# A chain of two transformer blocks on one Trainium2 core: gated linear attention normalises each head as it ends, the delta rule masks its first two groups earlier, and the last feed-forward starts its second product one chunk sooner

## The chip, the cores and the metric

The kernel runs on one core of one Trainium2 chip. The metric is the device time of one execution in microseconds (us), as the median of the runs shown. "About no change" below means within 0.2% of the time before.

## The reference

One sequence of 256 tokens, width 1024, float32, goes through two blocks. The first block is two layers: dilated window attention with a gated feed-forward ("layer a"), then gated linear attention with a gated feed-forward ("layer b"). The second block ("layer c") is attention beside a bidirectional gated delta rule, and a feed-forward with a convolution of three taps over the tokens. Three of these parts matter here.

```python
# layer b, for each of 4 heads (keys 128 wide, values 256), chunks of 64 tokens, forwards and backwards
o = chunked_linear_attention(q * exp(b), k * exp(-b), v)        # + states carried from chunk to chunk
y = rms_norm(o, out_norm) * silu(r)                             # norm over the 256 values of a head
h = h + y @ w_out
# layer c, delta rule: (I + A)^-1 of each 128 x 128 block, by levels of 2, 4, ... 64
# layer c, feed-forward
u = dwconv_centred(h @ w_up, conv_w, conv_b);  g, val = split(u);  h = (silu(g) * val) @ w_down
```

## The kernel before, in words

The program is written out by hand for each engine: TensorE (PE), VectorE (DVE), ScalarE (ACT), GpSimd (POOL) and SyncE (SP), whose queue loads the weights. Every engine runs its own list in order, and semaphores with fixed counts connect the lists. What order of work an engine has is therefore what is written in the code.

**Weights.** Every weight matrix is cut into halves of 128 x 2048 float32 (two 512 KB transfers each). A half is loaded into one of four slots `raw`, ACT copies it rounded to a short format into one of three slots `whi` (`Weights.hi`, L191), DVE subtracts the two into `wlo` (`Weights.lo`, L197), and PE multiplies with both (L326 to L328: three products for one). A slot is filled again when PE has signalled `used` for the half that stood in it. SP issues the loads.

**Layer b.** `project_pe/act/dve` make q, k, v and r (ACT applies silu to r while it takes it from PSUM, L1372) and the decays e1, e2, e3. Then `heads_pe/act/dve` run over the 4 heads. For head h, DVE makes `qd, kd, ke` (six products of 128 x 256, L1510 to L1512). PE transposes `ke` (L1445) and makes the scores (L1451), then works on a chunk of the modulation weights that has nothing to do with the head (`M.acc`, L827 and L828, 16 matmuls of 512 columns), then the products of keys and values of the chunks (L1464) and a few small ones (`M.cols`, L842). DVE masks the scores (L1519), carries the states over the chunks (L1527, L1530), makes `wlo` for the two halves that come next (L197), and once PE has made the head's output (L1472, L1478) copies it from PSUM to `o` (L1540). ACT copies the transposes (L1492), the row of the modulation product (L835), and the two halves (L191).

After the fourth head comes the gate (`gate_act`, `gate_dve`): a square over all of `o` (L1552), a sum over each head (L1559), a root (L1554), a reciprocal, and three products over 128 x 2048 (L1565 by the scale, L1567 by the gain, L1569 by silu(r)). Then PE transposes the result (L408) and multiplies by the output weights.

**Delta rule** (`gdn_heads`). It has two phases of four groups. For each group DVE makes the matrix N (its last step is L2398), POOL multiplies it by the mask of the first level (L2502), and DVE makes the first X with `first` (L2405). Then `levels` goes over 24 steps: `level_masks` on DVE makes two masked copies of a group's X (L2411, L2412), PE transposes one (L2220) and makes two products, with a third masked matrix that POOL makes (L2524), and DVE subtracts. Step s works on group s mod 4.

**Feed-forward** (`ffn`, used in all three layers). The first product runs over 11 chunks; chunk ci uses PSUM banks 0 to 3 if ci is even, 4 to 7 if it is odd. DVE ends each with `val` (L753), counted in `ff_val`, and splits it into `hid` (ACT L721, DVE L756). Then the second product ("down") runs over 6 double halves into banks 4, 5 and then 6, 7. In layer c, and there alone, the argument `beside` is None: nothing is done by PE between the two products.

## Time and profile before

| | |
|---|---|
| median of 3 runs | 1881.06 us (1879.68 to 1881.2) |
| profiled execution: its own time | 1878.88 us |
| its span in the trace | 1877.3 us |
| PE matmul busy | 1693.8 us (90%) |
| DVE busy | 1139.8 us (61%) |
| ACT busy | 863.8 us (46%) |
| POOL busy | 243.8 us (13%) |

How to read it: the span is from the first instruction to the last. The 1.58 us between it and the execution's own time lie around it. The busy time of PE is a model of pipelined matmuls, so a busy PE need not be PE at its fastest: the column PEclk (granted clock) says at which share of 2.4 GHz it ran.

### The profile page before, as it was taken

The page shows a single profiled execution, that of the slowest core. Times are in us where ns is not written, and L with a number is a line of the kernel's source. Part 1 is how long each engine was busy: PE and PEld are TensorE (multiplying, and loading weights), DVE is VectorE, ACT ScalarE, POOL GpSimd, SP SyncE. Part 2 cuts the span into 40 slices and gives each one's busy share as a digit, 9 for nine tenths or more (in the row PEclk, how much of TensorE's full clock was granted, in tenths as well). Part 3 has the DMA queues.
Part 4 walks back from the last instruction along what each step waited for, and adds up shares of the span by engine and source line. Part 5 has one row for each costly group of instructions (what it writes and reads, how often), then busy time and mean ns, then how long its engine had stood idle before and what let it go on. Part 6 is the DMA issues. An engine that isn't in the chain of part 4 may idle for free. (4 is left out here: it accounts for less than half of the span.)

```text
span 1877.3 us, 25093 instructions
## 1 busy us (share of the span) xinstructions
PE 1693.8 (90%) x10106; PEld 1472.9 (78%) x10106; DVE 1139.8 (61%) x1464; ACT 863.8 (46%) x1059; POOL 243.8 (13%) x205
## 2 busy tenths in 40 slices
PE   4999999989999987589999999988979899989988
PEld 3777888879987865479988678767879878779976
DVE  3887666755554454645546775347887565567754
ACT  5344556644433553244444423364544554345542
POOL 1653240000000000000000610004444100000000
PEclk9999999989999998799999999988989899989999
DMA  5552445645555343146645404100000155445533
GB/s 201 173 177 98 135 133 181 202 128 180 185 167 195 127 157 122 58 157 183 191 155 168 137 1 138 45 17 1 1 1 1 46 181 179 157 146 179 178 126 123
DMA packets 161906, 240.97 MB, mean 128 GB/s; under 512 B 12640, under 2 KB 80992, under 8 KB 161664
## 3 DMA queue, kind: packets, MB, share of 16 engines
q1 hardware_dynamic: 154400, 232.81, 38.1%
q10 hardware_dynamic: 7104, 4.64, 0.9%
q8 instruction: 81, 1.33, 0.3%
q0 software_dynamic: 288, 1.92, 0.3%
q14 instruction: 33, 0.27, 0.0%
HBM read 238.29 MB, written 1.05 MB: 127 GB/s over the span
## 5 line engine op out<-in xcount | busy, mean ns | idle before, releaser
L197 DVE TENSOR_TENSOR wlo<-raw,whi 128x2048 fp32r<-128x2048 f32 x224 | 524.3, 2352 | 309.3 <-ACT whi L191 298.8
L191 ACT ACTIVATE whi<-raw 128x2048 fp32r<-128x2048 f32 x224 | 420.4, 1887 | 302.3 <-PE ps L328 258.1
L326 PE MATMUL ps<-xs,whi 128*128 128x256 f32 (+1 forms) x1312 | 387.4, 295 | 18.3 <-DVE xs L460 7.7
L327 PE MATMUL ps<-xs,whi 128*128 128x256 f32 (+1 forms) x1312 | 386.0, 294 | 0.0
L328 PE MATMUL ps<-xs,wlo 128*128 128x256 f32 (+1 forms) x1312 | 385.8, 294 | 0.0
L326 PE MATMUL ps<-whi,xs 128*128 128x512 f32 x672 | 275.8, 410 | 19.0 <-DVE wlo L197 11.2
L326 PEld LDWEIGHTS ps<-xs,whi 128*128 128x128 f32 x1312 | 250.1, 191 | 27.2 <-issue 20.7
L327 PE MATMUL ps<-wlo,xs 128*128 128x512 f32 x672 | 270.7, 403 | 0.0
L328 PE MATMUL ps<-whi,xs 128*128 128x512 f32 x672 | 270.1, 402 | 0.0
L327 PEld LDWEIGHTS ps<-xs,whi 128*128 128x128 f32 x1312 | 250.2, 191 | 5.7
L328 PEld LDWEIGHTS ps<-xs,wlo 128*128 128x128 f32 x1312 | 250.0, 191 | 5.8
L326 PEld LDWEIGHTS ps<-whi,xs 128*128 128x128 f32 x672 | 129.8, 193 | 53.0 <-issue 21.1
L328 PEld LDWEIGHTS ps<-whi,xs 128*128 128x128 f32 x672 | 129.2, 192 | 32.1
L327 PEld LDWEIGHTS ps<-wlo,xs 128*128 128x128 f32 x672 | 129.7, 193 | 29.2
L326 PE MATMUL ps<-whi,hid 128*128 128x512 f32 x264 | 106.0, 402 | 8.7 <-DVE wide L753 8.7
L327 PE MATMUL ps<-wlo,hid 128*128 128x512 f32 x264 | 105.4, 399 | 0.0
L328 PE MATMUL ps<-whi,hid 128*128 128x512 f32 x264 | 105.4, 399 | 0.0
L1673 POOL TENSOR_TENSOR wide<-cst,wide 128x128 f32<-128x128 f32 x4 | 3.5, 870 | 765.5 <-DMA wide<-in_rows 765.5
L928 POOL TENSOR_TENSOR wide<-wide 128x512 f32<-128x512 f32 (+1 forms) x30 | 54.0, 1822 | 132.0 <-DVE wide L915 83.3
L933 POOL TENSOR_TENSOR wide<-wide 128x512 f32<-128x512 f32 (+1 forms) x30 | 67.8, 2281 | 2.6 <-DVE wide L915 1.7
L326 PEld LDWEIGHTS ps<-whi,hid 128*128 128x128 f32 x264 | 50.2, 190 | 21.2 <-DVE wide L753 9.1
L328 PEld LDWEIGHTS ps<-whi,hid 128*128 128x128 f32 x264 | 50.2, 190 | 12.3
(366 smaller groups left out, 2394.3 us busy)
## 6 DMA issues: line engine op xcount, KB each, us to landing
raw<-in_ffn_w_gate_up SPq DMA_DIRECT2D x88, 512.0 KB, 4.7
raw<-in_a_w_in SPq DMA_DIRECT2D x72, 512.0 KB, 4.6
raw<-in_w_in SPq DMA_DIRECT2D x60, 512.0 KB, 4.6
raw<-in_w_mod SPq DMA_DIRECT2D x48, 512.0 KB, 4.6
raw<-in_w_up SPq DMA_DIRECT2D x44, 512.0 KB, 4.7
raw<-in_ffn_w_down SPq DMA_DIRECT2D x40, 512.0 KB, 4.5
raw<-in_b_w_in SPq DMA_DIRECT2D x24, 512.0 KB, 4.6
raw<-in_w_down SPq DMA_DIRECT2D x20, 512.0 KB, 4.1
```

What stands on the lines that cost most here:

```text
L191: self.hi_ok.inc(act.activation(self.whi[:, h % NHI, 0:nk, :], self.raw[:, h % NRAW, 0:nk, :], ACT.Copy))
L197: self.lo_ok.inc(dve.tensor_tensor(self.wlo[:, h % NRAW, 0:nk, :], self.raw[:, h % NRAW, 0:nk, :], self.whi[:, h % NHI, 0:nk, :].bitcast(F ...
L326: pe.matmul(o, ahi, bhi, start=start, stop=False)
L327: pe.matmul(o, ahi, blo, start=False, stop=False)
L328: return pe.matmul(o, alo, bhi, start=False, stop=stop)
L928: i_ = pool.tensor_tensor(self.av[:, t], self.xv[:, t], bc(cos[:, t, :], 1, self.nh), ALU.mult)
L933: i_ = pool.tensor_tensor(dst(t), self.av[:, t], dst(t) if self.bv is None else self.bv[:, t], ALU.add)
L1673: pool.tensor_tensor(tab[:, 0, t, :], cosv[:, t, :], gain, ALU.mult)
```

## The change

There are three edits.

1. Layer b. The three arrays `qd, kd, ke` get two buffers each. `scale_qk(0)` is made during the projections, and `scale_qk(h + 1)` directly after the states of head h, in front of the `wlo` splits. The head's output is no longer copied to `o`: ACT squares it straight from PSUM with a running sum (2 instructions of 128 x 256 a head) and takes the root, DVE takes the reciprocal and makes one product from PSUM with the scale and with r (2 of 128 x 256 a head), into r itself. The gain is multiplied into r before, by POOL, in two instructions. The whole gate after the heads is gone.
2. Delta rule. In each phase `level_masks` for steps 0 and 1 stand in front of the last `first` and no longer behind it.
3. Feed-forward of layer c. In front of the second product PE waits for `val` of the tenth chunk, not of the eleventh.

```diff
-            pe.wait_ge(ff_val.sem, v0 + N_FFC)
+            pe.wait_ge(ff_val.sem, v0 + N_FFC - (beside is None))
...
+        def scale_qk(h):
+            hs = slice(h * SEQ, (h + 1) * SEQ)
+            qd, kd, ke = qd_[h % 2], kd_[h % 2], ke_[h % 2]
+            for d in range(2):
+                dve.tensor_tensor(qd[:, d, :], qT[:, h, :], e1[:, d, hs], ALU.mult)
+                dve.tensor_tensor(kd[:, d, :], kT_[:, h, :], e2[:, d, hs], ALU.mult)
+                i_ = dve.tensor_tensor(ke[:, d, :], kT_[:, h, :], e3[:, d, hs], ALU.mult)
+            lb_qk.inc(i_)
...
-            for h in (*later[4], *later[5]):
+            for h in later[4]:
+                W.lo(h)
+            dve.wait_ge(lb_ex.sem, 1)
+            dve.wait_ge(lb_evac.sem, 2)
+            scale_qk(0)
+            for h in later[5]:
                 W.lo(h)
...
+                for t in range(TT):
+                    act.wait_ge(lb_o.sem, 2 * h + t + 1)
+                    as_.inc(act.activation(sq[:, t], ps[:, 6 + t, 0:GLA_DV], ACT.Square, scale=GLA_DV ** -0.5, accum_out=st[:, h, t:t + 1]))
+                act.wait_ge(as_.sem, as_.n)
+                lb_rt.inc(act.activation(st[:, h], st[:, h], ACT.Sqrt, bias=eps_col))
+
+        def heads_pool():
+
+            pool.wait_ge(rows_in.sem, rows_at)
+            for j in range(2):
+                pool.wait_ge(lb_evac.sem, 5 + j)
+                half = slice(j * CW, (j + 1) * CW)
+                lb_gr.inc(pool.tensor_tensor(r[:, :, half], r[:, :, half], bc(gain[:, half], 1, TT), ALU.mult))
...
+                if h + 1 < GLA_HEADS:
+                    scale_qk(h + 1)
+                M.out(8 + h, 5)
                 for half in nxt[h]:
                     W.lo(half)
-                M.out(8 + h, 5)
+                dve.wait_ge(lb_rt.sem, h + 1)
+                vs.inc(dve.reciprocal(st[:, h], st[:, h]))
+                dve.wait_ge(vs.sem, vs.n)
+                dve.wait_ge(lb_gr.sem, 1 + h // 2)
                 for t in range(TT):
-                    dve.wait_ge(lb_o.sem, 2 * h + t + 1)
-                    lb_out.inc(dve.tensor_copy(o[:, t, hv], ps[:, 6 + t, 0:GLA_DV]))
+                    lb_out.inc(dve.scalar_tensor_tensor(r[:, t, hv], ps[:, 6 + t, 0:GLA_DV], st[:, h, t:t + 1], r[:, t, hv],
+                                                        ALU.mult, ALU.mult))
...
-        gate_act()
-        gate_dve()
-        split_and_add(lambda t, k: o[:, t, k * P:(k + 1) * P], 0, out_chunks, nxt_chunk, norm)
+        heads_pool()
+        split_and_add(lambda t, k: r[:, t, k * P:(k + 1) * P], 0, out_chunks, nxt_chunk, norm)
...
                 if Gn % 4 == 3:
+                    if ph == 0:
+                        dve.wait_ge(gm_in.sem, 16)
+                    dve.wait_ge(gp_x.sem, 4 * ph + 2)
+                    level_masks(ph, 0)
+                    level_masks(ph, 1)
                     first(Gn)
```

VectorE before, between the outputs of head 1 and the masked scores of head 2 (L1530 ends the states, L197 are the splits of the next weights, L1540 the copies to `o`, L1510 to L1512 the six products that head 2 needs):

```order
L1530 SCALAR_TENSOR_TENSOR wide<-wide,ps 128x256 [waits s_dve_steps] x2
L197 TENSOR_TENSOR wlo<-raw,whi 128x2048 [waits s_hi_ok,s_raw_in0]
L197 TENSOR_TENSOR wlo<-raw,whi 128x2048 [waits s_hi_ok,s_raw_in1]
L851 TENSOR_TENSOR gcol<-ps,vec 128x4 [waits s_mod_cols]
L1540 COPY wide<-ps 128x256 [waits s_b_product] x2
L1510 TENSOR_TENSOR wide<-wide 128x256 [waits s_b_product]
L1511 TENSOR_TENSOR wide<-wide 128x256
L1512 TENSOR_TENSOR wide<-wide 128x256
```

VectorE in the changed kernel at the same kind of place, from the end of one head's states to the next head's masked scores (here L1387 to L1389 are the products, L1569 the product from PSUM into r):

```order
L1554 SCALAR_TENSOR_TENSOR wide<-wide,ps 128x256 [waits s_dve_steps] x2
L1387 TENSOR_TENSOR wide<-wide 128x256
L1388 TENSOR_TENSOR wide<-wide 128x256
L1389 TENSOR_TENSOR wide<-wide 128x256
L1387 TENSOR_TENSOR wide<-wide 128x256
L1388 TENSOR_TENSOR wide<-wide 128x256
L1389 TENSOR_TENSOR wide<-wide 128x256
L854 SCALAR_TENSOR_TENSOR modcol<-ps,vec 128x8 [waits s_mod_cols]
L197 TENSOR_TENSOR wlo<-raw,whi 128x2048 [waits s_hi_ok,s_raw_in2]
L197 TENSOR_TENSOR wlo<-raw,whi 128x2048 [waits s_hi_ok,s_raw_in3]
L1565 RECIPROCAL wide<-wide 128x2 [waits s_b_root]
L1569 SCALAR_TENSOR_TENSOR wide<-ps,wide 128x256 [waits s_b_gain,s_dve_steps]
```

The products for the next head have moved in front of the two splits and no longer wait for the head's output; the wait for ACT's root stands in front of the next head's masked scores.

VectorE before, at the end of the fourth head and in the gate (L1559 to L1569), up to the split of the result into `xs` (L453):

```order
L851 TENSOR_TENSOR gcol<-ps,vec 128x4 [waits s_mod_cols]
L1540 COPY wide<-ps 128x256 [waits s_b_product] x2
L1559 TENSOR_REDUCE wide<-wide 128x8 [waits s_rope_out,s_b_out,s_b_squares,s_mod_rows,s_b_product]
L1562 RECIPROCAL wide<-wide 128x8 [waits s_rows_in,s_b_root]
L1565 TENSOR_TENSOR wide<-wide 128x2048 [waits s_dve_steps]
L1567 TENSOR_TENSOR wide<-wide 128x2048 [waits s_dve_steps]
L1569 TENSOR_TENSOR wide<-wide 128x2048 [waits s_dve_steps]
L453 TENSOR_TENSOR xs<-ps,xs 128x512 [waits s_rope_out,s_dve_steps,s_xs_hi,s_b_root,s_b_product]
```

The same place in the changed kernel:

```order
L851 TENSOR_TENSOR gcol<-ps,vec 128x4 [waits s_mod_cols]
L197 TENSOR_TENSOR wlo<-raw,whi 128x2048 [waits s_hi_ok,s_raw_in2]
L197 TENSOR_TENSOR wlo<-raw,whi 128x2048 [waits s_hi_ok,s_raw_in3]
L1565 RECIPROCAL wide<-wide 128x2 [waits s_b_root]
L1569 SCALAR_TENSOR_TENSOR wide<-ps,wide 128x256 [waits s_b_gain,s_dve_steps]
L1569 SCALAR_TENSOR_TENSOR wide<-ps,wide 128x256
L453 TENSOR_TENSOR xs<-ps,xs 128x512 [waits s_b_gain,s_b_out,s_xs_hi,s_b_root,s_b_product]
```

Four instructions over 2048 elements are gone from between the last output and the split; a reciprocal and two of 256 elements stand there.

VectorE in the changed kernel at the end of the second phase's (and likewise the first phase's) preparation in the delta rule (L2402 ends N, L2414 is `first`, L2420 and L2421 are the level masks):

```order
L2402 TENSOR_TENSOR wide<-wide,spare 128x512 [waits s_dve_steps,s_gdn_scales]
L2420 TENSOR_TENSOR spare<-wide 128x512 [waits s_gdn_x_first,s_gdn_masks_in]
L2421 TENSOR_TENSOR spare<-wide 128x512
L2420 TENSOR_TENSOR spare<-wide 128x512
L2421 TENSOR_TENSOR spare<-wide 128x512
L2414 TENSOR_TENSOR wide<-cst,wide 128x512 [waits s_gdn_n_first]
L2420 TENSOR_TENSOR spare<-wide 128x512 [waits s_gdn_u,s_gdn_x_first]
```

Before, the last `first` (L2405 there), with its wait for POOL, stood directly behind N, and all the masks behind it.

## Rows read from the trace of the kernel before

**Rows 1.** The page, busy time of each engine and its instructions.
```profile
PE 1693.8 (90%) x10106; PEld 1472.9 (78%) x10106; DVE 1139.8 (61%) x1464; ACT 863.8 (46%) x1059; POOL 243.8 (13%) x205
```

**Rows 2.** Waits of PE: us in total, times, longest.
```profile
PE ps L2220 <- DVE spare L2412: 17.7, 2, 9.9
...
PE ps L1445 <- DVE wide L1512: 15.2, 4, 5.0
PE ps L408 <- DVE wide L1569: 14.0, 1, 14.0
```

**Rows 3.** Timeline of PE, heads: start, us, instruction, [idle before].
```profile
699.56 0.95 PE L1445 MATMUL ps<-cst,wide 128*128 128x128 f32 x4 [5.05 <-DVE wide L1512]
...
739.00 1.12 PE L1445 MATMUL ps<-cst,wide 128*128 128x128 f32 x4 [3.78 <-DVE wide L1512]
...
741.47 0.77 PE L827 MATMUL ps<-whi,by_hi 128*128 128x512 f32 x1
...
746.49 2.75 PE L1464 MATMUL ps<-wide 128*128 128x256 f32 x12
...
752.20 0.67 PE L1472 MATMUL ps<-wide 128*128 128x256 f32 x2 [2.18 <-issue]
...
754.45 1.08 PE L1478 MATMUL ps<-wide 128*64 128x256 f32 x6
```

**Rows 4.** Timeline of DVE, end of head 2.
```profile
751.10 1.00 DVE L1530 SCALAR_TENSOR_TENSOR wide<-wide,ps 128x256 f32<-128x256 f32 x2
752.02 4.49 DVE L197 TENSOR_TENSOR wlo<-raw,whi 128x2048 fp32r<-128x2048 f32 x2
...
757.16 0.41 DVE L1510 TENSOR_TENSOR wide<-wide 128x256 f32<-128x256 f32 x1
...
758.83 0.42 DVE L1512 TENSOR_TENSOR wide<-wide 128x256 f32<-128x256 f32 x1
```

**Rows 5.** ACT: two timeline rows of layer b, one group by form.
```profile
694.55 1.02 ACT L1372 ACTIVATE wide<-ps 128x1024 f32<-128x1024 f32 x1 [3.62 <-PE ps L328]
...
782.14 0.30 ACT L1554 ACTIVATE wide<-wide,small 128x8 f32<-128x8 f32 x1 [1.15 <-DVE wide L1559]
...
L431 ACT ACTIVATE xs<-ps,vec 128x256 fp32r<-128x256 f32 x24 | 9.0, 482 | 0.0
```

**Rows 6.** Timeline of DVE and PE, end of head 3 and gate.
```profile
772.39 4.49 DVE L197 TENSOR_TENSOR wlo<-raw,whi 128x2048 fp32r<-128x2048 f32 x2
...
789.91 3.65 PE L408 MATMUL ps<-cst,wide 128*128 128x128 f32 x16 [14.02 <-DVE wide L1569]
```

**Rows 7.** Timeline of DVE, PE and ACT, between the feed-forward's products, layer c.
```profile
1795.08 4.49 DVE L197 TENSOR_TENSOR wlo<-raw,whi 128x2048 fp32r<-128x2048 f32 x2 [1.12 <-ACT whi L191]
...
1804.48 0.79 PE L326 MATMUL ps<-whi,hid 128*128 128x512 f32 x1 [7.32 <-DVE wide L753]
...
1806.99 2.29 DVE L197 TENSOR_TENSOR wlo<-raw,whi 128x2048 fp32r<-128x2048 f32 x1 [1.11 <-ACT whi L191]
...
1812.53 1.92 ACT L191 ACTIVATE whi<-raw 128x2048 fp32r<-128x2048 f32 x1 [5.64 <-PE ps L328]
1818.15 1.91 ACT L191 ACTIVATE whi<-raw 128x2048 fp32r<-128x2048 f32 x1 [3.70 <-PE ps L328]
```

**Rows 8.** Timeline of DVE and POOL, ends of the delta rule's preparations.
```profile
1284.81 1.56 DVE L2405 TENSOR_TENSOR wide<-cst,wide 128x512 f32<-128x512 f32 x1 [1.21 <-POOL wide L2502]
...
1287.79 0.68 DVE L2412 TENSOR_TENSOR spare<-wide 128x512 f32<-128x512 f32 x1
...
1377.38 1.57 DVE L2412 TENSOR_TENSOR spare<-wide 128x512 f32<-128x512 f32 x1
...
1284.73 2.59 POOL L2524 TENSOR_TENSOR spare<-wide,cst 128x512 f32<-128x512 f32 x2
```

**Rows 9.** Windows: start:end, length, busy and count per engine, PEclk, DMA share, GB/s.
```profile
714.00:717.00 3.00, 2.94 (x8) 1.10 (x8) 2.69 (x5) 0.00 (x0) 0.00 (x0) 0.53 0.00 1
...
732.00:735.00 3.00, 3.00 (x16) 1.41 (x16) 3.00 (x2) 0.00 (x0) 0.00 (x0) 1.00 0.14 53
```

More of the change, by code:

```diff
@@ L1274, in build @@
     lb_g, lb_ke, lb_att, lb_kv, lb_o = (Signal(nc, "pe", "b_" + n) for n in ("gates", "ke_transposed", "scores", "kv", "product"))
-    lb_ln, lb_ex, lb_evac, lb_kt, lb_sq = (Signal(nc, "act", "b_" + n) for n in ("gate_ln", "decays", "evacuated", "kt", "squares"))
-    lb_qk, lb_at, lb_s, lb_out, lb_sum = (Signal(nc, "dve", "b_" + n) for n in ("qk_scaled", "masked", "states", "out", "sum"))
+    lb_ln, lb_ex, lb_evac, lb_kt = (Signal(nc, "act", "b_" + n) for n in ("gate_ln", "decays", "evacuated", "kt"))
+    lb_qk, lb_at, lb_s, lb_out = (Signal(nc, "dve", "b_" + n) for n in ("qk_scaled", "masked", "states", "out"))
+    lb_gr = Signal(nc, "pool", "b_gain")
     lb_rt = Signal(nc, "act", "b_root")
@@ L1324, in layer_b @@
         dec = c(2, NB)
+        qd_, kd_, ke_ = ([c(2, SEQ) for _ in range(2)] for _ in range(3))
         at_ = Stage()
@@ L1505, in heads_dve @@
             for h in range(GLA_HEADS):
-                hs, hv = slice(h * SEQ, (h + 1) * SEQ), slice(h * GLA_DV, (h + 1) * GLA_DV)
+                hv = slice(h * GLA_DV, (h + 1) * GLA_DV)
                 if h:
                     dve.wait_ge(lb_o.sem, 2 * h)
-                for d in range(2):
-                    dve.tensor_tensor(qd[:, d, :], qT[:, h, :], e1[:, d, hs], ALU.mult)
-                    dve.tensor_tensor(kd[:, d, :], kT_[:, h, :], e2[:, d, hs], ALU.mult)
-                    i_ = dve.tensor_tensor(ke[:, d, :], kT_[:, h, :], e3[:, d, hs], ALU.mult)
-                lb_qk.inc(i_)
                 dve.wait_ge(lb_att.sem, h + 1)
```

30 lines of the change are left out of this document (2 added, 28 removed).

## The prediction

> **What bounds the kernel now.** I read the page first: PE is busy for 90% of the span [rows 1], so time can be won only where PE stands still or runs at half clock. Then the list of PE's waits, which names the places of this change: the masks of the delta rule (17.7 us in two waits, the longest 9.9), the six products in front of each head (15.2 us in four), the gate behind the heads (14.0 us) [rows 2]; the wait in front of the second product of the last feed-forward, 7.32 us, is read from the timeline [rows 7]. Last I read the timelines around each to see what DVE does while PE waits, and how late each following instruction would be.
>
> In layer b one head takes PE 20.3 us: transposes and scores 739.00 to 741.47, the modulation chunk to 746.49, keys times values and a wait of 2.18 us to 752.20, outputs to 755.53 (754.45 + 1.08), and 3.78 us of waiting for L1512 [rows 3]. In that last wait DVE finishes the splits it began at 752.02, copies the output and makes the six products, 757.16 to 759.25 [rows 4].
>
> **Head start.** The products of head 0 are now made before the last two splits of the projections. PE's list may go on when ACT has evacuated r, at 695.57 (694.55 + 1.02) [rows 5]; it started at 699.56 [rows 3]. I take 695.7, so 3.9 us earlier.
>
> **One head.** The six products (2.1 us, 757.16 to 759.25) stand directly behind the states, which end at 752.0 [rows 4]. They are ready at 754.1, before the outputs end at 755.53, so the 3.78 us are gone and PE goes from outputs to transposes in about 0.1. Without that gap I also expect more full clock: the 16 modulation matmuls took 5.0 us (741.47 to 746.49) with the gap ahead of them; 24 matmuls of the same size at full clock take 5.62 us (between the two ACT rows that wait for PE, 1812.53 and 1818.15 [rows 7]), 0.234 each, so 16 take 3.75. Transposes and scores took 2.47 at half clock; at full clock half of it, 1.24. I take the middle, 1.85, since some of it may still be slow. From keys times values to the outputs stays 5.71 (746.49 to 752.20), the outputs 3.33. Sum: 0.1 + 1.85 + 3.75 + 5.71 + 3.33 = 14.7 us in place of 20.3.
>
> What must keep up in these 14.7 us? Call A the end of a head's outputs; the states end at A - 3.5. DVE: products to A - 1.4, the small L854, two splits (4.5) to A + 3.2, reciprocal and two products from PSUM of about 0.5 each to A + 4.5, masked scores 1.0 to A + 5.5. Its next input, keys times values of the next head, ends at A + 0.1 + 1.85 + 3.75 + 2.75 = A + 8.4, so 2.9 us are left. The next modulation chunk wants the first new `wlo` at A + 2.0 and has it at A + 1.0, the second at A + 3.8 and has it at A + 3.2. ACT: a square of 128 x 256 from PSUM costs 0.48 [rows 5], the root 0.30, so with reading out the sum the root is there at about A + 1.2, and the copy of the transposes behind it is done some 3 us before keys times values need it; the table for roots is now loaded in head 0 and no longer in the gate. DMA moves next to nothing in stretches of the loop (share 0.00 and 0.14 [rows 9]), so weights are not what would be late.
>
> **POOL's two products with the gain.** They are new, and no row shows 128 x 1024 on POOL. Two of 128 x 512 take 2.59 us beside DVE [rows 8], so 2.6 each is my value; free would be the lower bound, and twice, 5.2, the upper. The first lies under the projections, the second starts at 695.6, when DVE clears its buffers. If DVE has to stand for it, the copy of the transposes is 2.6 us late, and it has 4 us of modulation matmuls as cover. Cost taken: 0; with 5.2 us it would be about 1.5.
>
> **Gate.** PE's gap after the last output is 14.02 us [rows 6]. What remains: the splits started 3.5 before A (772.39 against 775.89) and with the small operation ahead of them end at A + 1.1; root at A + 1.2; reciprocal 0.2, two products of 0.5, so PE starts at A + 2.7.
>
> Put together: last outputs at 695.7 + 4 x 14.7 = 754.5, transposes at 757.2 in place of 789.91: 32.7 us. From this I take one fall of the clock: in the four heads before, the 2.2 us gap that remains was followed by half clock once (714 to 717, clock 0.53) and not in head 1 (732 to 735, clock 1.00) [rows 9]; 3 us at 0.53 lose 1.4. The restart after a gap of 2.7 in place of 14 may keep some full clock, +0.4. Layer b: **31.7 us**, with bounds of 24 (a fall in every head, -5.6, and the POOL cost) and 35.
>
> **Delta rule.** DVE waited 1.21 us for POOL and then made `first` in 1.56, because POOL worked beside it; alone such an operation takes 0.68 [rows 8]. Now the masks use that wait. In phase 1 the first pair was complete at 1287.79 + 0.68 = 1288.5; it now starts at 1283.6 and with one of the two slowed is complete at 1285.9. But all eight masks of the first four steps and `first` are still DVE's work, POOL has the same three operations, and more of DVE's now fall beside them. So the first step starts 2.5 us earlier, the fourth hardly; PE's own steps decide what remains. I take 1.2 us. In phase 2 the first pair ended at 1379.0 (1377.38 + 1.57) and both of it were slowed; it loses the same wait and `first` ahead of it (1.21 + 1.56), so it would end near 1376.2, and PE's second step, which stood behind it, follows. I take 2.1. Together **3.3 us**, bounds 0 and 6.
>
> What speaks against this edit is the meeting of the two engines: the rows say 1.56 against 0.68 us for a DVE operation with two inputs beside POOL [rows 8]. The Trainium skill, page "SBUF — State Buffer", section on the two separate sides, says that such a DVE instruction and a GpSimd instruction that reads SBUF take a shared port pair as an exclusive lock for the whole instruction. By that rule every mask moved beside POOL waits out one POOL instruction and POOL in turn waits for it, and the edit gives nothing; the trace agrees so far as 1.56 is nearly one operation of each.
>
> **Feed-forward of layer c.** The second product's banks 4 and 5 are free after the tenth chunk. PE now starts at once, at about 1797.4: its last matmul ended at 1797.16 (1804.48 - 7.32), and the first split half was ready at 1797.3 (half of 1795.08 to 1799.57) [rows 7]. Two halves at 5.62 take it to 1808.7. The third half's `wlo` is ready at 1809.3 (1806.99 + 2.29), which does not depend on PE, so PE waits 0.6. Before, the third half began at 1818.1. That is **8.7 us**: 7.3 of waiting and 2.0 of half clock after it, less the new wait. Below: 7.0, if the clock falls again. The eleventh chunk's `hid` is wanted only by the fifth half, long after.
>
> **Sum.** 31.7 + 3.3 + 8.7 = 43.7 us. The profiled execution would go from a span of 1877.3 to 1833.6 and from 1878.88 to 1835.2; it lay 2.2 us under the median of the runs, so I forecast 1881.06 - 43.7 = **1837 us**.
>
> **Rivals.**
> - The clock, 0.15. PE falls to half clock after the remaining gap in every head and keeps it through the modulation chunk as now. For it: half clock at 714; against: full clock at 732 with the same gap [rows 9]. Each head then takes about 16.3 us: 1844 us.
> - The shared port, 0.10. DVE and POOL stop each other wherever they meet: the delta rule gains 0 and layer b pays 1.5. 1842 us.
> - DVE takes over as the bound of a head, 0.08. The reciprocal waits for ACT's root in front of the next masked scores. If DVE's list were 3 us longer than I count, its slack of 2.9 would be used up; if it were 6 us longer, three heads would lose about 3 us each: 1846 us.
> - Slower than before, 0.03. ACT's squares now stand behind the rounding of the next two halves, and DVE and the next head behind them. If a half lands late, both engines and PE stand, where before only the modulation chunk did. To turn 43.7 us of gain into a loss of over 3.8, each of four heads must be held 12 us, so halves would land more than 25 us after their slot came free. Against it: DMA shares of 0.00 and 0.14 [rows 9]. It would give 1890 us.
> - The edits do nothing that counts, since other work fills the same time, 0.02: 1881 us. Against it: PE has no other instruction before these waits.
> - My forecast, 0.62: 1832 to 1842.
>
> Within 0.2% (3.8 us) is what a measurement of this kernel can't tell from no change. The range 1830 to 1850 takes in the forecast, the first three rivals and a layer b that keeps clock fully. Faster 0.95, same 0.02, slower 0.03.
>
> **What would show it.** In the trace after: L1461 (the transposes of heads 1 to 3) starts within 0.2 us of the outputs' end, with a period near 14.7 us and DVE idle in front of L1551; PE's gap before L408 near 2.7; masks beside POOL at 1.5 us and PE's first level step 2 to 3 us after N; in the feed-forward no wait in front of the second product and one of about 0.6 in front of its third half. I am wrong if the period stays over 16.5, if the gap before L408 is over 5, or if the second product waits more than 3 us for its third half.

## The result and the profile after

The changed kernel takes 1834.8 us (median of 4 runs, 1830.42 to 1864.69) against 1880.37 us of the kernel before (4 runs, 1876.53 to 1881.2). The ratio is 0.9753, with a 95% interval of 0.9739 to 0.9767; the run of 1864.69 us had a disturbed clock and is not in the ratio. The profiled execution took 1835.56 us with a span of 1833.9 us, 43.4 us less than the span of before. The forecast was 1837 us, and the result lies in its range of 1830 to 1850.

The page's busy line, which answers to [rows 1]:

```profile
PE 1683.5 (92%) x10106; PEld 1462.5 (80%) x10106; DVE 1135.5 (62%) x1463; ACT 867.2 (47%) x1077; POOL 250.9 (14%) x207
```

PE executes the same 10106 matmuls, in 10.3 us less of busy time. So about a quarter of the 43.4 us is matmuls that ran at the faster clock; the rest is standing time. The list of PE's waits (us in total, times, longest) answers to [rows 2]:

```profile
PE ps L2224 <- DVE spare L2421: 14.5, 4, 6.2
...
PE ps L1488 <- issue: 6.5, 3, 2.2
...
PE ps L408 <- DVE wide L1569: 2.2, 1, 2.2
...
PE ps L326 <- DVE wide L753: 1.4, 1, 1.4
```

The 15.2 us for the six products are gone from it altogether, the 14.0 us of the gate are 2.2, the wait for L753 fell from 8.7 in two to 1.4 in one. The delta rule's wait is still there: 17.7 us in two waits have become 14.5 us in four.

**Heads.** Timeline of PE (start, us, instruction, idle before), which answers to [rows 3]: rows from heads 0 to 2 and the outputs of head 3.

```profile
697.59 0.63 PE L1461 MATMUL ps<-cst,wide 128*128 128x128 f32 x4 [1.16 <-issue]
...
713.24 0.66 PE L1461 MATMUL ps<-cst,wide 128*128 128x128 f32 x4
...
714.54 0.48 PE L827 MATMUL ps<-whi,by_hi 128*128 128x512 f32 x1
...
724.08 0.67 PE L1488 MATMUL ps<-wide 128*128 128x256 f32 x2 [2.18 <-issue]
724.68 1.08 PE L1494 MATMUL ps<-wide 128*64 128x256 f32 x6
...
727.33 0.66 PE L1461 MATMUL ps<-cst,wide 128*128 128x128 f32 x4
...
753.95 1.19 PE L1488 MATMUL ps<-wide 128*128 128x256 f32 x2 [2.18 <-issue]
...
758.13 1.97 PE L1494 MATMUL ps<-wide 128*64 128x256 f32 x6
```

L1461, the transposes, has no idle time before it in heads 1 to 3: PE goes from outputs to transposes at once. Head 1 ran at full clock throughout and took 727.33 - 713.24 = 14.09 us. What remains is the gap of 2.2 us before L1488, in which PE waits for the states. Behind it the same outputs take 3.25 us in head 1 (724.08 to 727.33) and 6.15 us in head 3 (753.95 to 758.13 + 1.97 = 760.10), since the groups are nearly twice as long there: 1.97 in place of 1.08 is half clock.

**DVE and POOL at the start.** Timeline of DVE and of POOL, around the products of head 0 and the clearing of the buffers, with the reciprocal at the end of head 0:

```profile
685.42 2.61 DVE L1387 TENSOR_TENSOR wide<-wide 128x256 f32<-128x256 f32 x1
687.96 0.41 DVE L1388 TENSOR_TENSOR wide<-wide 128x256 f32<-128x256 f32 x1
...
697.67 0.27 DVE L1529 MEMSET wide<- 128x256 f32 x1 [2.42 <-ACT wide L1374]
...
715.48 0.17 DVE L1565 RECIPROCAL wide<-wide 128x2 f32<-128x2 f32 x1 [0.70 <-ACT wide L1517]
...
685.19 2.56 POOL L1525 TENSOR_TENSOR wide<-wide 128x1024 f32<-128x1024 f32 x1 [411.09 <-ACT wide L1374]
697.57 2.38 POOL L1525 TENSOR_TENSOR wide<-wide 128x1024 f32<-128x1024 f32 x1 [9.82 <-ACT wide L1374]
```

The first product began 0.23 us after POOL's and took 2.61 us, its neighbour 0.41: it stood until POOL had ended. The clearing beside POOL's second product took its 0.27 us and was not held. The reciprocal of head 0 waited 0.70 us for ACT's root; in this head ACT loads the table for the root first, which takes it 1.28 us.

**Gate.** DVE and PE after the last output (at 760.10), which answers to [rows 6]:

```profile
760.99 0.17 DVE L1565 RECIPROCAL wide<-wide 128x2 f32<-128x2 f32 x1 [2.67 <-ACT wide L1517]
761.19 0.88 DVE L1569 SCALAR_TENSOR_TENSOR wide<-ps,wide 128x256 f32<-128x256 f32 x2
...
762.32 2.57 PE L408 MATMUL ps<-cst,wide 128*128 128x128 f32 x16 [2.22 <-DVE wide L1569]
```

**Delta rule.** DVE and PE after the last N of phase 1 (which ends at 1251.06) and of phase 2 (1341.30), which answers to [rows 8]:

```profile
1250.98 0.68 DVE L2420 TENSOR_TENSOR spare<-wide 128x512 f32<-128x512 f32 x1
1251.58 1.58 DVE L2421 TENSOR_TENSOR spare<-wide 128x512 f32<-128x512 f32 x1
...
1253.31 1.09 PE L2224 MATMUL ps<-cst,spare 128*128 128x128 f32 x4 [5.06 <-DVE spare L2421]
1256.22 1.12 PE L2224 MATMUL ps<-cst,spare 128*128 128x128 f32 x4 [1.82 <-DVE spare L2421]
1257.13 1.92 PE L2231 MATMUL ps<-spare 128*128 128x128 f32 x8
...
1262.69 0.69 DVE L2453 TENSOR_TENSOR wide<-wide,ps 128x512 f32<-128x512 f32 x1 [3.39 <-PE ps L2239]
...
1343.55 1.09 PE L2224 MATMUL ps<-cst,spare 128*128 128x128 f32 x4 [6.20 <-DVE spare L2421]
...
1353.43 0.69 DVE L2453 TENSOR_TENSOR wide<-wide,ps 128x512 f32<-128x512 f32 x1 [0.54 <-PE ps L2239]
```

The same places in the kernel before, where the last N ends at 1283.60 and 1373.20:

```profile
1288.62 2.23 PE L2220 MATMUL ps<-cst,spare 128*128 128x128 f32 x8 [7.82 <-DVE spare L2412]
1290.64 1.92 PE L2227 MATMUL ps<-spare 128*128 128x128 f32 x8
...
1295.40 0.69 DVE L2448 TENSOR_TENSOR wide<-wide,ps 128x512 f32<-128x512 f32 x1 [3.17 <-PE ps L2235]
...
1386.69 0.69 DVE L2448 TENSOR_TENSOR wide<-wide,ps 128x512 f32<-128x512 f32 x1 [1.34 <-PE ps L2235]
```

The first pair of masks is complete 2.1 us after N (1253.16 against 1251.06), where it took 4.9 us before (1288.47 against 1283.60). Three of the four masks that were moved take 1.58 us (two of them, at 1253.09 and 1254.59, are not shown), since each meets POOL. L2448, which is L2453 after, is the subtraction that ends a step.

**Feed-forward.** DVE and PE between the products, which answers to [rows 7]:

```profile
1760.04 4.49 DVE L197 TENSOR_TENSOR wlo<-raw,whi 128x2048 fp32r<-128x2048 f32 x2 [1.11 <-ACT whi L191]
...
1771.97 6.69 DVE L197 TENSOR_TENSOR wlo<-raw,whi 128x2048 fp32r<-128x2048 f32 x3 [1.11 <-ACT whi L191]
...
1762.48 0.47 PE L326 MATMUL ps<-whi,hid 128*128 128x512 f32 x1 [0.33 <-DVE wlo L197]
...
1774.41 0.47 PE L326 MATMUL ps<-whi,hid 128*128 128x512 f32 x1 [0.45 <-DVE wlo L197]
```

The wait of 7.32 us is one of 0.33 us, and the new wait before the third half is there, with 0.45 us.

**By stages.** The span is cut at five instructions that all kernels have: the end of r's copy from PSUM (before 695.57, after 697.49), the first L408 behind the heads (789.91, 762.32), the ends of the last N of phase 1 and of phase 2 (1283.60 and 1373.20, 1251.06 and 1341.30), and the end of the last `val` in the last feed-forward. Each number is a difference of two such times in that kernel's one profiled execution, the last one up to the end of the span.

| kernel | to r | heads and gate | to N, phase 1 | phase 1 | to last val | to the end | span |
|---|---|---|---|---|---|---|---|
| before | 695.57 | 94.34 | 493.69 | 89.60 | 431.23 | 72.87 | 1877.3 |
| after | 697.49 | 64.83 | 488.74 | 90.24 | 428.09 | 64.51 | 1833.9 |
| e1, layer b alone | 695.42 | 67.57 | 493.08 | 89.60 | 431.18 | 72.85 | 1849.7 |
| e2, delta rule alone | 695.71 | 94.35 | 493.68 | 90.95 | 426.40 | 72.91 | 1874.0 |
| e3, feed-forward alone | 695.55 | 96.22 | 493.82 | 89.60 | 431.20 | 64.51 | 1870.9 |
| e5, products early alone | 697.43 | 78.21 | 492.48 | 89.75 | 434.07 | 73.26 | 1865.2 |
| e6, after, products late | 697.27 | 88.29 | 487.55 | 88.34 | 427.71 | 64.54 | 1853.7 |
| e7, after, gap filled | 694.79 | 54.60 | 491.72 | 90.30 | 428.08 | 64.51 | 1824.0 |
| e8, after, one mask pair | 696.03 | 64.72 | 490.80 | 89.57 | 428.34 | 64.54 | 1834.0 |
| e9, after, POOL five times | 694.27 | 73.47 | 491.90 | 90.30 | 428.10 | 64.46 | 1842.5 |
| e10, e7 and e8 | 693.98 | 54.60 | 491.14 | 89.35 | 431.20 | 64.53 | 1824.8 |

Two columns differ where no edit can be the cause. The third holds no edit, and differs by up to 6.3 us. The first holds of the edits only the products of head 0 and POOL's first product, from 685 us on, and differs by up to 3.5 us. What the changed kernel lost there, 1.9 us, it had lost by 112 us, 1.6 of it between two of ACT's L191 (8.80 us, 102.77 to 111.57, where before it was 7.25, 102.30 to 109.55), as PE's matmuls of 0.40 us took 0.63 there. So the early products cost nothing in front of r.

Windows show what differs in the third stage, for 25 us that begin at about the same instruction in both kernels (start:end, length, busy and count for PE, PEld, DVE, ACT, POOL, then granted clock, DMA share, GB/s), first before:

```profile
1065.00:1090.00 25.00, 19.48 (x88) 12.72 (x87) 20.33 (x35) 7.28 (x15) 14.58 (x11) 0.84 0.20 70
```

and after:

```profile
1037.00:1062.00 25.00, 17.93 (x98) 12.15 (x97) 21.03 (x37) 7.29 (x15) 14.33 (x10) 1.00 0.19 65
```

The clock was 0.84 there and 1.00 here. What that was worth is read between two instructions that stand around it: from the start of ACT's L191 at 1062.49 to the next one at 1119.50 it was 57.0 us before, from 1034.15 to 1088.55 it was 54.4 after, so 2.6 us. Another 1.6 us was won in the 84 us in front of the last N of phase 1 (84.5 against 82.9, at a granted clock of 0.90 and 0.92). The remaining 0.7 us is the restart behind the gate: the first L408 group takes 2.57 us in place of 3.65 [rows 6], 1.1 less, but within the next 10 us 0.4 of it is lost again. That makes the 4.95 us that this stage gained. With layer b alone (e1) the stretch from L191 to L191 takes 57.0 us again, with the early products alone (e5) 56.1, with products late (e6) 54.4. It goes with none of the edits in an orderly way, and I count these 4.2 us as luck of the clock.

### The profile page after: what moved, and what is told of

It reads as the page before. It is cut to its first block and busy times, and to the rows that moved or that the text cites. A ratio compares the mean times of both kernels' runs of the same rounds, so it can differ in the third digit from the quotient of the medians.

```text
span 1833.9 us, 25119 instructions
## 1 busy us (share of the span) xinstructions
PE 1683.5 (92%) x10106; PEld 1462.5 (80%) x10106; DVE 1135.5 (62%) x1463; ACT 867.2 (47%) x1077; POOL 250.9 (14%) x207
## 5 line engine op out<-in xcount | busy, mean ns | idle before, releaser
L197 DVE TENSOR_TENSOR wlo<-raw,whi 128x2048 fp32r<-128x2048 f32 x224 | 524.1, 2352 | 298.9 <-ACT whi L191 288.4
L191 ACT ACTIVATE whi<-raw 128x2048 fp32r<-128x2048 f32 x224 | 420.6, 1888 | 294.9 <-PE ps L328 250.9
L1525 POOL TENSOR_TENSOR wide<-wide 128x1024 f32<-128x1024 f32 x2 | 4.9, 2466 | 420.9 <-ACT wide L1374 420.9
L328 PEld LDWEIGHTS ps<-whi,hid 128*128 128x128 f32 x264 | 49.7, 188 | 12.1
```

Source lines behind the costliest of these rows:

```text
L191: self.hi_ok.inc(act.activation(self.whi[:, h % NHI, 0:nk, :], self.raw[:, h % NRAW, 0:nk, :], ACT.Copy))
L197: self.lo_ok.inc(dve.tensor_tensor(self.wlo[:, h % NRAW, 0:nk, :], self.raw[:, h % NRAW, 0:nk, :], self.whi[:, h % NHI, 0:nk, :].bitcast(F ...
L328: return pe.matmul(o, alo, bhi, start=False, stop=stop)
L1525: lb_gr.inc(pool.tensor_tensor(r[:, :, half], r[:, :, half], bc(gain[:, half], 1, TT), ALU.mult))
```

## The experiments

**One edit each.** Three kernels take the change apart. e1 is the changed kernel with the other two edits undone:

```diff
-            pe.wait_ge(ff_val.sem, v0 + N_FFC - (beside is None))
+            pe.wait_ge(ff_val.sem, v0 + N_FFC)
...
-                    if ph == 0:
-                        dve.wait_ge(gm_in.sem, 16)
-                    dve.wait_ge(gp_x.sem, 4 * ph + 2)
-                    level_masks(ph, 0)
-                    level_masks(ph, 1)
                     first(Gn)
...
                 dve.wait_ge(gp_x.sem, 4 * ph + 4)
+                if ph == 0:
+                    dve.wait_ge(gm_in.sem, 16)
+                level_masks(ph, 0)
+                level_masks(ph, 1)
```

> The kernel before with the edit of layer b alone (nothing left out of the computation). Theory: nearly all of the gain is here. By the prediction's terms 31.7 us (1880.4 to about 1848.7); by the trace after, where the stretch from the end of r's evacuation to the transposes behind the gate is 64.8 us and was 94.3, 29.5 us there and 1 to 2 us of restart at full clock, 31. Rival (the DVE list or the shared port takes the gain back): 20 to 24 us. Three heads with half clock cost 1.6 to 2.9 us each in the trace after; I expect two to four of them again.

Measured: 1851.41 us, ratio 0.9856 (0.9837 to 0.9876), so 27.1 us (23.3 to 30.6). The heads and the gate took 67.57 us in place of 94.34, a gain of 26.8, and the restart kept 0.6 us of the third stage. That is 27.4, between the 31 of my theory and the 20 to 24 of the rival. The clock makes the difference to the changed kernel: here the outputs ran partly or wholly at half clock in all four heads (4.80, 4.85, 6.08 and 6.15 us, where the changed kernel has 4.80, 3.25, 4.85 and 6.15), which is 2.8 us.

e2 is the kernel before with the masks moved, and nothing else:

```diff
                 if Gn % 4 == 3:
+                    if ph == 0:
+                        dve.wait_ge(gm_in.sem, 16)
+                    dve.wait_ge(gp_x.sem, 4 * ph + 2)
+                    level_masks(ph, 0)
+                    level_masks(ph, 1)
                     first(Gn)
...
-                if ph == 0:
-                    dve.wait_ge(gm_in.sem, 16)
-                level_masks(ph, 0)
-                level_masks(ph, 1)
```

> The kernel before with the edit of the delta rule alone. The prediction's term was 3.3 us. The trace after speaks for less: the masks beside POOL took 1.57 us each, and the first phase, from the end of its last N to the end of the second phase's last N, took 90.2 us after and 89.6 before. So I now expect phase 1 to gain nothing (0 to -1) and phase 2 to gain 0 to 2: 0 to 1.5 us in all. The rival, my term of 3.3, would show as 1877.

Measured over 12 runs: 1875.92 us against 1878.94, ratio 0.9983 (0.9973 to 0.9993), so 3.2 us (1.3 to 5.1). So the time speaks for the 3.3 us of the prediction and not for the 0 to 1.5 that I expected here. By stages phase 1 took 1.35 us longer, and the stage with phase 2 4.8 us less. The first subtraction of a step came 0.5 us sooner behind N in phase 1 (11.27 against 11.80) and 2.0 us sooner in phase 2 (11.51 against 13.49); the rest of both differences lies later, where the granted clock differs.

e3 is the kernel before with the one wait changed:

```diff
-            pe.wait_ge(ff_val.sem, v0 + N_FFC)
+            pe.wait_ge(ff_val.sem, v0 + N_FFC - (beside is None))
```

> The kernel before with the earlier start of the last feed-forward's second product alone. The prediction's term: 8.7 us (7.3 of waiting, 2.0 of half clock, less a new wait of 0.6). Rival: the split of the third half ends later than PE reaches it by more than 3 us, and the gain is under 6.

Measured: 1872.21 us, ratio 0.9966 (0.9953 to 0.9979), so 6.4 us (3.9 to 8.8). Its own stage went from 72.87 to 64.51 us, 8.36 less, just as in the full change; 1.9 us were lost in heads and gate, where e3 has no edit.

The three add to 36.7 us and the full change is worth 46.4 us by its ratio ((1 - 0.9753) x 1880.37, 43.8 to 49.1). By their spans it is 37.3 against 43.4. The table shows where the other 6.1 us lie: the full change has 4.5 us more in the third stage than the three together and 4.6 more in heads and gate (29.5 against 26.8 in e1 and -1.9 in e3), 0.7 more in phase 1, and 1.9 and 1.8 less in the first stage and the one with phase 2. Where I read the rows, the clock accounts for them: one more head with slow outputs in e1 (2.8 us), half clock in the modulation chunk of head 0 in e3 (5.23 us in place of 4.39) and in the heads behind it, and the stretches of the third stage named above. So one profile's clock moves a stage by up to some 5 us.

**Layer b taken apart.** e5 is the kernel before with the products for the next head made early, in two buffers, and the old copy and gate kept:

```diff
+        def scale_qk(h):
+            ...
...
-        qd, kd, ke = c(2, SEQ), c(2, SEQ), c(2, SEQ)
+        c(6, SEQ)
...
                     lb_s.inc(i_)
+                if h + 1 < GLA_HEADS:
+                    scale_qk(h + 1)
+                M.out(8 + h, 5)
                 for half in nxt[h]:
                     W.lo(half)
-                M.out(8 + h, 5)
```

The old place of the six products stays reserved in e5. Without that (e4) `xs` shares a place with an array that PE still reads when DVE writes `xs`, so its result would hang on the timing, and it has no time.

> The kernel before with one part of the layer b edit: the six products are made ahead, in two buffers; the copies to o and the whole gate behind the heads stay. By rows 3 and 4: 3.9 us at the start, and 3.7 of waiting plus up to 1.9 of full clock for each of three heads, while the gate's 14.0 us stay: the stretch from r's evacuation to the transposes, 94.3 us before, would be 75 to 78, and the time 1880 less 16 to 20. Rival: the copies to o, behind the splits, hold PE's outputs, and the gain is under 12.

Measured: 1866.78 us, ratio 0.9928 (0.991 to 0.9947). That is 13.5 us by the ratio and 12.1 by the spans, where I expected 16 to 20. Heads and gate took 78.21 us, 16.1 less than before and at the edge of the expected 75 to 78; the other 4 us were lost where nothing is changed: 1.9 in front of r and 2.8 behind phase 1, less 1.2 won in the third stage. The timeline of PE in e5:

```profile
760.89 1.97 PE L1494 MATMUL ps<-wide 128*64 128x256 f32 x6
775.64 3.65 PE L408 MATMUL ps<-cst,wide 128*128 128x128 f32 x16 [12.78 <-DVE wide L1582]
```

The heads end at 762.86, so they took 65.4 us from r, where they took 80.3 before (775.89 - 695.57); the gate's gap is still 12.78 us.

e6 is the opposite: the changed kernel with its new normalisation, but the products at their old place behind the outputs.

```diff
                 if h:
                     dve.wait_ge(lb_o.sem, 2 * h)
+                    scale_qk(h)
...
-                if h + 1 < GLA_HEADS:
-                    scale_qk(h + 1)
```

> The changed kernel with the products for heads 1 to 3 made at their old place, behind the head's output and the new product into r; head 0's stay early. Theory: the gate's part of the gain stays (11 to 12 us) and the start (3.9), the per-head part goes and is more than gone, since the next products now also stand behind ACT's root: PE's gap in front of a head's transposes 4.5 to 5.5 us, where it was 3.8. Stretch 94.3 less 13 to 16, so 78 to 81; the time of the changed kernel plus 14 to 17. Rival: the gap is hidden and the time is within 5 us of the changed kernel.

Measured: 1858.28 us, ratio 0.9882 (0.9861 to 0.9902), with heads and gate at 88.29 us, 7 to 10 us more than I had expected (20 us more than the changed kernel by the spans, where I had 14 to 17). The timelines of PE and DVE in e6, head 1 to head 2, show why:

```profile
733.96 1.82 PE L1494 MATMUL ps<-wide 128*64 128x256 f32 x6
739.81 1.11 PE L1461 MATMUL ps<-cst,wide 128*128 128x128 f32 x4 [4.03 <-DVE wide L1389]
...
736.67 0.17 DVE L1564 RECIPROCAL wide<-wide 128x2 f32<-128x2 f32 x1 [1.43 <-ACT wide L1517]
...
737.66 0.42 DVE L1387 TENSOR_TENSOR wide<-wide 128x256 f32<-128x256 f32 x1
```

The products stand behind the wait for ACT's root, which did not exist before, so PE's gap is 4.03 us (5.31 behind head 0) in place of 3.78 [rows 3] (2.54 behind head 0). That adds 3.3 us, about as expected. What I had not counted is the outputs: they took 4.89, 4.91, 6.14 and 6.16 us, where before they took 4.91 and three times 3.32 or 3.33, so 7.2 us more at half clock.

So the per-head normalisation takes 11.8 us from the gate's gap, and the heads take 86.1 us (697.27 to 783.35) in place of 80.3, although e6 keeps the early start of head 0, which is worth 3.9. The two parts of the edit need each other. Early products alone bring 16.1. Normalisation with only the early start of head 0 brings 6.1, which leaves 2.2 for the normalisation itself. Both together bring 29.5, and 16.1 + 2.2 is 18.3.

**The gap that remains.** In e7 the second half of each modulation chunk stands behind keys times values, so that PE has work while DVE carries the states:

```diff
-                for s in range(2):
-                    M.acc(8 + h, s, 5)
+                M.acc(8 + h, 0, 5)
                 pe.wait_ge(lb_kt.sem, h + 1)
...
                     lb_kv.inc(i_)
+                M.acc(8 + h, 1, 5)
                 M.cols(8 + h, 5, rows)
```

> The changed kernel with the second half of each head's modulation chunk moved behind the products of keys and values, into the 2.2 us in which PE waits for the states. Theory A: that gap is the last wait of the loop and it is also what lets the clock fall (three of four heads in the trace after). Then a head takes 12.0 to 12.6 us in place of 14.1 (full clock) and 15.7 to 17 (with a fall), and the stretch 64.8 becomes 52 to 58: 7 to 12 us faster. Theory B: DVE (11.7 us of work a head) becomes the bound, or the row of the modulation product, now later on ACT, holds the outputs: no more than 3 us faster.

Measured: 1827.53 us (1825.47 to 1829.41), ratio 0.972 (0.97 to 0.9739). That is 6.2 us less than the changed kernel by the ratios, whose intervals just touch, and 9.9 us by the spans. Timeline of PE in e7, head 1 to head 2, and its window over all heads:

```profile
716.34 1.05 PE L842 MATMUL ps<-cst,wide 128*128 128x2 f32 x8 [0.69 <-ACT wide L835]
...
720.52 0.66 PE L1461 MATMUL ps<-cst,wide 128*128 128x128 f32 x4
...
694.00:748.00 54.00, 48.41 (x256) 35.66 (x256) 42.53 (x82) 27.79 (x42) 2.37 (x1) 1.00 0.54 176
```

and the window over the heads of the changed kernel:

```profile
697.00:760.00 63.00, 53.65 (x256) 38.19 (x256) 42.58 (x82) 27.21 (x39) 2.38 (x1) 0.89 0.45 150
```

The same 256 matmuls take 48.41 us in place of 53.65. A wait of 0.69 us for ACT's row stands where 2.2 us stood, and the clock stayed at 1.00 through all four heads. A head takes 12.7 to 12.9 us (694.89, 707.59, 720.52, 733.24). That is a little over the 12.0 to 12.6 of theory A, and the stretch of 54.60 us lies inside its 52 to 58. Heads and gate gained 10.2 us, of which 4 x 1.5 = 6.0 are gap and 5.2 busy time; the gate's gap gave 1.1 back (3.34 us in place of 2.22).

The gap of 2.2 us is not the whole cause of the slow outputs. Outputs without a fall take 3.3 us; count as slow those of 4.6 us or more. With the gap and early products, they were slow in 16 heads of 20 (3, 4, 4, 3 and 2 of four in the changed kernel, e1, e5, e8 and e9), with the gap and late products in all four of e6, and without it in none of eight (e7, e10). But in the kernel before, e2 and e3, which have the same gap of 2.2 us, they were slow in 2 heads of 12. What held the clock up there is open.

**Delta rule, one pair.** e8 is the changed kernel with only the first step's masks ahead of `first`:

```diff
                     level_masks(ph, 0)
-                    level_masks(ph, 1)
                     first(Gn)
+                    level_masks(ph, 1)
```

> The changed kernel with the masks of step 0 alone in front of the last first, those of step 1 behind it. In the trace after, three masks ran beside POOL at 1.57 us, and in phase 1 the second pair was complete 5.7 us after N, where before it was 6.1. Theory: with one pair ahead the first step keeps its early start and phase 1 gets back the 0.6 to 1.4 us that it lost; phase 2 stays: 0 to 1.5 us faster. Rival: first, which waits for POOL's first product, then holds the second pair, and it is 0 to 1 us slower.

Measured: 1837.04 us, ratio 0.9784 (0.9762 to 0.9807), which overlaps the changed kernel's interval. By the ratios it is 5.8 us slower and by the spans the same (1834.0 against 1833.9), and the profile is of the fastest of its five runs; so the time does not show the 0 to 1.5 us that I expected. In the trace phase 1 is back at 89.57 us and the stage with phase 2 keeps its gain (428.34). Windows of 10 us, 60 us behind the last N of phase 1, when the levels end: before, after, e8.

```profile
1343.60:1353.60 10.00, 8.23 (x58) 7.30 (x57) 7.96 (x13) 4.76 (x13) 0.00 (x0) 1.00 0.01 3
```

```profile
1311.10:1321.10 10.00, 8.24 (x51) 7.45 (x50) 7.27 (x12) 4.55 (x12) 0.00 (x0) 0.83 0.01 2
```

```profile
1311.50:1321.50 10.00, 8.24 (x58) 7.31 (x58) 7.96 (x13) 4.74 (x13) 0.00 (x0) 1.00 0.01 2
```

With both pairs ahead the clock fell to 0.83 at the end of the phase (0.73 in e2), which is 10 x 0.17 = 1.7 us of full clock, of which the phase shows 0.6 to 0.7 us; with one pair the clock stays at 1.00. e7, e9 and the changed kernel have both pairs and a phase 1 of 90.2 to 90.3 us, e8 and e10 one pair and 89.4 to 89.6. But e6 has both pairs too, and its phase 1 took 88.34 us. So the loss goes with a fall of the clock that is usual with both pairs and not bound to them. Up to the first subtraction, the second pair gains little: this came 11.63 us after N with both pairs and 11.78 with one in phase 1, 12.13 and 12.74 in phase 2. How much of that is clock stays open.

**The shared port.** e9 puts four more POOL products, into an array that nothing reads, in front of each of the two real ones:

```diff
                 half = slice(j * CW, (j + 1) * CW)
+                for _ in range(4):
+                    gs.inc(pool.tensor_tensor(pz, r[:, :, half], bc(gain[:, half], 1, TT), ALU.mult))
+                    pool.wait_ge(gs.sem, gs.n)
```

> The changed kernel with four additional POOL products (128 x 1024, result into a scratch array that nothing reads) in front of each of the two real gain products, so POOL works about 12.8 us twice, from 685.2 and from 697.6, where before it worked 2.6 us twice. Theory A (a two-input DVE instruction on SBUF and a POOL instruction never overlap, each stands for one whole instruction of the other): the six products of head 0 and the split behind them alternate with five POOL instructions and end 10 us or more later, PE then waits for wlo, and the same again in head 0 or 1 for the second batch: 12 to 22 us in all, 1847 to 1857 us. Each of the first five DVE products shows about 2.5 us. Theory B (POOL only slows what DVE reads by some share, or only the first meeting costs): products of 0.41 stay under 1 us, PE's waits stay as they were, 1835 to 1838 us.

Measured: 1844.96 us, ratio 0.9824 (0.9808 to 0.984). By the ratios that is 13 us more than the changed kernel ((0.9824 - 0.9753) x 1880), by the spans 8.6, all of it in heads and gate (73.47 against 64.83). Timeline of DVE and POOL in e9:

```profile
683.76 2.63 DVE L1388 TENSOR_TENSOR wide<-wide 128x256 f32<-128x256 f32 x1
...
696.44 2.56 DVE L1390 TENSOR_TENSOR wide<-wide 128x256 f32<-128x256 f32 x1
698.92 8.81 DVE L197 TENSOR_TENSOR wlo<-raw,whi 128x2048 fp32r<-128x2048 f32 x2
707.73 0.27 DVE L1533 MEMSET wide<- 128x256 f32 x1
...
709.29 1.03 DVE L1547 COPY_PREDICATED wide<-cst,ps 128x128 f32<-128x128 int32 x4
...
683.52 10.22 POOL L1527 TENSOR_TENSOR wide<-wide 128x1024 f32<-128x1024 f32 x4 [411.17 <-ACT wide L1375]
...
696.19 13.80 POOL L1527 TENSOR_TENSOR wide<-wide 128x1024 f32<-128x1024 f32 x4
```

All six products take 2.56 to 2.63 us, not 0.41, one POOL product each, and two splits take 8.81 in place of 4.49. POOL pays too: four products take 10.22 us beside the short DVE instructions and 13.80 beside the long ones. The clearing (0.27) and the masking from PSUM (1.03, as without POOL, and partly beside it) are not held. That is theory A in its mechanism. Its price was at or below the lower end of my 12 to 22 us. By chance fewer outputs were slow (4.91, 3.33, 3.32 and 4.91 us, together 2.6 less than in the changed kernel), so I estimate the delay itself at 8.6 + 2.6 = 11.2 us. Part of it met slack: PE waited 5.99 us for the last product, 1.50 and 0.62 for splits, and 0.65 for ACT. By this the Trainium skill, page "SBUF — State Buffer", section on the two separate sides, is borne out: it calls the shared pair "an exclusive lock, not a bandwidth split" for a DVE instruction with two SBUF inputs against a GpSimd instruction that reads SBUF. The one product that met POOL in the changed kernel (2.61 us) follows the same rule.

**Both good edits.** e10 is e7 with e8's order of the masks; its edits are those two.

> The changed kernel with two edits that were measured one at a time: the second half of the modulation chunk behind keys times values, and only the first pair of level masks in front of the last first. If they add: the ratio of the first, 0.972, and from the second only the 0.7 us that phase 1 of the delta rule had lost, so 1826 to 1828 us by the time of 1827.5 for the first alone, with phase 1 at 89.6 us and heads and gate together at 54.6 us in the trace. The rival: a kernel that was faster in the head part starts the delta rule at another clock, and the second edit is hidden by that; then phase 1 stays near 90.3 and the time at 1827.5 or above.

Measured: 1827.94 us (1826.44 to 1831.64), ratio 0.9732 (0.9716 to 0.9747), the same as e7 within their intervals. Phase 1 took 89.35 us and heads and gate 54.60, as they should have if the edits add, but the stage with phase 2 took 431.20 in place of 428.34. It lost about 3 us of clock there: in the windows of 20 us from the last N, the clock was 0.68 in the first in place of e8's 0.76, 0.91 in the fifth in place of 1.00. So whether the second edit is worth 0.7 us in the time is not settled; it is smaller than what the clock gives and takes.

## Why the prediction was right, and where it was not

**Layer b, forecast 31.7 us: right in mechanism, 1.5 us too high here and 4.3 in e1.** Measured: 94.34 - 64.83 = 29.5 in the stage, and 0.7 that the restart kept behind it, 30.2. With the edit alone (e1) it was 27.4, and by its time 27.1 (23.3 to 30.6), which leaves 31.7 out. Step by step:
- The start after r's copy: 0.1 us behind it (697.59 against 697.49), as forecast. The products of head 0 were not late, although one of them stood behind POOL.
- The gap before the transposes: 0, as forecast. Transposes and scores took 1.30 us (713.24 to 714.54); I had taken the middle, 1.85, and full clock was right in all four heads: 2.2 us too pessimistic. The modulation matmuls took 3.82 us (3.75 forecast).
- The one fall of the clock, 1.4 us, is the term that was mis-sized. The outputs took 4.80, 3.25, 4.85 and 6.15 us in the four heads; against 3.25 without a fall that is 6.05 us. The falls come after the 2.2 us gap in three heads of four, and they hit the outputs. So did the one at 714 before [rows 9], which lies in head 0's outputs (712.02 to 716.93) and not in its modulation chunk. So the clock rival, with 0.15 the largest, was half right: falls in nearly every head, of 2.0 us in the mean, but they were over before the modulation chunk. e7 and e10 show what the gap has to do with it: with it filled none of eight heads has a fall. I took one fall because the trace before had one in four heads; that the same gap would be followed by so many more in the changed kernel no row of before showed, and why is open.
- Together: 4.65 us more for the clock (6.05 - 1.4), 2.2 less for transposes and scores, so the heads took 62.6 us (697.49 to 760.10), where I had 60.2.
- DVE was not the bound: it stood 5.20, 3.66, 2.95 and 4.44 us in front of L1551, where I had computed 2.9. In heads 0 and 3 it waited for the root, 0.70 us (behind the load of the table) and 2.67 us; in the last that was until 0.9 us after the outputs (760.99 - 760.10), where I had computed 1.2.
- Gate: 2.22 us against 2.7. The terms that I gave add to 2.4, and PE starts 0.25 us after DVE's last product (762.07 to 762.32), which was not among them. Both products from PSUM took 0.88 us together and not 1.0, and the root came sooner. The restart kept 0.7 us where I had put 0.4.
- The lower bound of 24 counted the one fall twice; its own terms give 26 (31.7 less three more falls of 1.4 and the 1.5 of POOL).
- Weights were not late, as forecast, but not for the reason given: the DMA share over the heads was 0.45, where the two stretches of 3 us that I had read showed 0.00 and 0.14 [rows 9]. ACT's copies of the halves (L191) followed the row of the modulation product without a wait in every head.
- POOL's products: 2.56 and 2.38 us (2.6 forecast), cost 0 as taken. The second one met only clearing and masking, which it does not hold.

**Delta rule, forecast 3.3 us: right in sum, partly by luck, and wrong in its parts.** e2 gives 3.2 us (1.3 to 5.1), the stages of the changed kernel 2.5. I had put 1.2 us on phase 1 and 2.1 on phase 2. What the masks bring is read at the first subtraction of a step, since the steps behind it keep their distance to it.
- Phase 1: 0.2 us (11.80 us after N before, 11.63 after; in e2 0.5). The first transposes did start 2.8 us sooner against N (5.02 and 2.25). But PE's list has the transposes of the second step in front of the first product, and for these it stood 1.82 us, since the second pair of masks met POOL twice. So the first product came only 1.0 us sooner (7.04 and 6.07). The rest went to the clock: PE ran at half of it until 10.0 us after N before and until 10.7 after. The phase then lost 0.6 us (1.35 in e2) in all, with the fall of the clock at its end.
- Phase 2: 1.4 us (13.49 and 12.13; in e2 2.0). The first 10 us behind N hold 6.15 us of PE work in place of 4.10, but at another clock (0.71 against 0.54). The other 1.8 us of that stage's 3.1 lie behind the first subtraction and come with the clock.
- The rival of the shared port was right that the engines stop each other (three of four moved masks at 1.58 us). It was nearly right for phase 1, and wrong that nothing is gained in phase 2: the first pair needs only one of these meetings.

**Feed-forward, forecast 8.7 us: right.** 8.36 us in the changed kernel and in e3. The difference is the 0.33 us before the second product, which I had at 0; the wait before the third half is 0.45 against 0.6, and the clock from 1760 to 1785 was 1.00, where it was 0.50 between 1804 and 1809 before. By its time e3 gives 6.4 us (3.9 to 8.8): the 8.36 of its stage less the 1.9 that the clock took in the heads.

**The sum.** The three terms measured 30.2 + 2.5 + 8.4 = 41.1 us where I had 43.7. The span fell by 43.4. The other 2.3 us came from code without an edit, which lost 1.9 us ahead of r and won 4.2 in the third stage by its clock. The three edits measured one at a time add to 36.7 us only. So the forecast of 1837 us was met within 3 us with every term somewhat too high, the clock's share above all, and with luck of the clock elsewhere that made up for it.

## What to carry to other kernels

A gap of PE costs its length and, often, as much again in half clock behind it: here the last 2.2 us per head cost 1.55 to 2.9 us more in three heads of four (though in only 2 of 12 heads of the kernels with the old order), so a gap is worth filling with unrelated matmuls even when it looks small. A normalisation that is moved into a loop brings a wait for another engine with it; it pays only if what the next iteration needs stands in front of that wait (6.1 us without, of which 3.9 are head 0's early start, and 29.5 us with). In a kernel of this length, effects below 3 us are read from the rows of their stage and from counts of waiting and busy time, not from the time alone.

## What the runs showed of the hardware

- A DVE instruction with both inputs in SBUF and a POOL instruction of the same kind do not overlap: 0.41 us became 2.56 to 2.63 us behind a POOL product, and 2.24 us became 4.4 (8.81 for two). DVE instructions that clear, or that read one of their inputs from PSUM, took their usual 0.27 and 1.03 us while POOL worked, the last for part of the time.
- POOL takes 2.37 or 2.38 us for a product of 128 x 1024 float32 where no DVE instruction with two inputs in SBUF stands beside it (at 710.07 in e9, 697.57 in the changed kernel), and 1.09 us for 128 x 512 (1283.68 before).
- The granted clock of the same, unchanged stretch of code differed between kernels: 0.84 and 1.00 over 25 us of the third stage. Between the two instructions around it that is 2.6 us, nearly as much as the whole edit of the delta rule (3.2).
- Squaring 128 x 256 from PSUM with a running sum took ACT 0.39 us and 0.20 us to read the sum out; changing the table for the root took 1.28 us, once, in head 0.
